# A two-block transformer kernel on one core: the low parts, taps and decays of both mixers in another order, and edits in attention, the first feed-forward head and the last norm

## The reference, cut to what matters

```
xn = rms_norm(h); z = xn @ w_in                       # first block
y_conf = silu(layer_norm(conv31(a * sigmoid(b)))) @ w_conf_pw
y_att  = forgetting_attention(q, k, v, f_logit)       # 4 heads, causal, decay by cumsum(log f)
y_sc   = sc_b * conv3(sc_c * sc_h);  y_pool = window means (2, 4, 8, 16) @ w_pool * scale
h = h + rms_norm(concat(y_conf, y_att, y_sc, y_pool) @ w_out)
h = h + rms_norm(square(relu(rms_norm(h) @ w_up)) @ w_down)          # "ff", 4096 wide
h = h + rms_norm((p @ w_ple_proj) * sigmoid(rms_norm(h) @ w_ple_gate))

x = x + attention_mixer(rms_norm(x))    # 8 latent heads and 4 pairs of differential maps
x = x + swiglu(rms_norm(x))             # "f0", 2816 wide
x = x + recurrent_mixer(rms_norm(x))    # chunked state space (8 heads) and gated linear recurrence (4 heads)
x = x + swiglu(rms_norm(x))             # "f1"
return rms_norm(x)
```

## Time and profile before

| | |
|---|---|
| median of 3 runs | 1001.95 us (999.59 to 1003.36) |
| the profiled execution's own time | 1000.06 us |
| its span (first to last instruction) | 998.2 us |
| TensorE busy | 953.5 us, 96% |
| VectorE, ScalarE, POOL busy | 700.3, 515.8, 87.1 us |
| DMA | 164.40 MB, mean 165 GB/s; the queue of the weights busy for 48.9% of 16 engines |
| a load of 1 MB (w_up, s_w_out), issue to landing | 5.6, 4.9 us |
| an output store of 256 KB | 2.1 us |
| mean granted TensorE clock | 0.992 of full |

### The profile page before, as it was taken

One profiled execution on the slowest core, in us unless ns is written; L12 is line 12 of the kernel. 1 busy time (PEld: TensorE's weight loads), 2 busy tenths in 40 slices (PEclk: granted clock), 3 DMA queues, 4 the chain that ended last, 5 costly groups with the idle time before them and its releaser, 6 DMA issues.

```text
span 998.2 us, 13575 instructions
## 1 busy us (share of the span) xinstructions
PE 953.5 (96%) x5540; PEld 835.9 (84%) x5540; DVE 700.3 (70%) x921; ACT 515.8 (52%) x698; POOL 87.1 (9%) x110
## 2 busy tenths in 40 slices
PE   6997999999999899889999999999989889999997
PEld 5996797888888688778988888888988789888886
DVE  4798785666667887886666666667979676666663
ACT  4776754444436646765543434368645355434341
POOL 4353000000000100000000000000132000000000
PEclk9999999999999999989999999999999999999999
DMA  9732365665565354224665656546321356656531
GB/s 320 245 128 92 120 220 194 199 207 183 174 206 175 112 171 143 85 85 125 215 208 173 207 171 209 169 149 211 127 85 49 121 169 211 207 172 208 172 127 43
DMA packets 106190, 164.40 MB, mean 165 GB/s; under 512 B 2816, under 2 KB 82784, under 8 KB 106000
## 3 DMA queue, kind: packets, MB, share of 16 engines
q1 hardware_dynamic: 104688, 158.25, 48.9%
q0 software_dynamic: 1440, 5.28, 1.5%
HBM read 162.47 MB, written 1.05 MB: 164 GB/s over the span
## 4 chain that ended last, share of the span: by engine, by line
PE 69%; DVE 19%; ACT 6%; issue 4%; DMA 2%; POOL 1%; DVEq 0%; POOLq 0%; ACTq 0%
PE ps L379 67%; DVE wl L1739 6%; DVE SC L1841 2%; PE ps L387 2%; ACT wh L1172 2%; DMA raw<-in_w_in 1%; DVE xhl L1744 1%; DVE xf L1748 1%; ACT junk L1160 1%; DVE st L2139 1%; ACT xhl L1178 1%; POOL st L2496 1%; DVE rows L2339 1%; DVE hs L1759 0%; DVE h L1801 0%
## 5 line engine op out<-in xcount | busy, mean ns | idle before, releaser
L1739 DVE TENSOR_TENSOR wl<-raw,wh 128x2048 fp32r<-128x2048 f32 (+2 forms) x150 | 339.6, 2266 | 153.8 <-ACT wh L1172 153.6
L1172 ACT ACTIVATE wh<-raw 128x2048 fp32r<-128x2048 f32 (+2 forms) x150 | 281.9, 1884 | 156.6 <-PE ps L379 142.8
L379 PE MATMUL ps<-xhl,wh 128*128 128x512 f32 (+1 forms) x1248 | 257.9, 354 | 2.5 <-ACT wh L1237 2.5
L379 PEld LDWEIGHTS ps<-xhl,wh 128*128 128x128 f32 x1248 | 202.4, 193 | 29.9 <-issue 3.7
L379 PE MATMUL ps<-wh,xhl 128*128 128x512 f32 (+3 forms) x1000 | 195.2, 339 | 6.0 <-ACT SC L1435 1.8
L379 PEld LDWEIGHTS ps<-wh,xhl 128*128 128x128 f32 x1000 | 155.1, 190 | 25.3 <-ACT xhl L1178 2.6
L379 PEld LDWEIGHTS ps<-xhl,wl 128*128 128x128 f32 x1008 | 135.6, 191 | 7.5
L379 PE MATMUL ps<-xhl,wl 128*128 128x256 f32 x1008 | 140.6, 282 | 0.0
L379 PE MATMUL ps<-wl,xhl 128*128 128x512 f32 (+3 forms) x500 | 105.2, 336 | 0.0
L379 PE MATMUL ps<-wh,fh 128*128 128x512 f32 x304 | 91.0, 392 | 1.8 <-DVE fl L1986 1.5
L379 PE MATMUL ps<-wh,fl 128*128 128x512 f32 x304 | 90.2, 390 | 0.0
(11 more groups left out here) (266 smaller groups left out, 840.8 us busy)
## 6 DMA issues: line engine op xcount, KB each, us to landing
raw<-in_ffn_gate SPq DMA_DIRECT2D x22, 1024.0 KB, 5.3
raw<-in_ffn_up SPq DMA_DIRECT2D x22, 1024.0 KB, 5.4
raw<-in_ffn_down SPq DMA_DIRECT2D x22, 1024.0 KB, 4.9
raw<-in_w_up SPq DMA_DIRECT2D x16, 1024.0 KB, 5.6
raw<-in_w_down SPq DMA_DIRECT2D x16, 1024.0 KB, 4.9
raw<-in_s_w_in SPq DMA_DIRECT2D x14, 1024.0 KB, 5.4
raw<-in_w_in SPq DMA_DIRECT2D x9, 1024.0 KB, 7.1
raw<-in_a_w_in SPq DMA_DIRECT2D x6, 1024.0 KB, 5.1
```

Of the source, the lines that this page charges most:

```text
L379: return e.matmul(o, a, b, start=start, stop=stop, skip_group_check=True)
L1172: e.activation(high_of(i), raw_of(i), ACT.Copy).then_inc(*up("act_high", i))
L1739: e.tensor_tensor(low_of(i), raw_of(i), high_of(i).bitcast(F32), ALU.subtract).then_inc(*up("dve_lo", i))
```

## The change

Nothing is computed otherwise except in two places: the copies of `xs` and `cbs` go from ScalarE to VectorE, and the last norm multiplies by the gain first and by the root second, the second half of the width on ScalarE. The rest moves steps within an engine's list and changes some waits:

- First mixer. ScalarE: `highs(10)` behind `forget_probs(0)` and `(1)`; taps 22 and 23 before them; the last taps before `forget_turned(0)`; the conformer's Sqrt before `forget_probs(3)`. VectorE: `lows(8)` behind the first maxima, `forget_inverse(0)` and `(1)` before taps 16 to 18, `lows(10)` behind all taps and behind `forget_max(3)`; the conformer's centring and square before `mix_low(3)`.
- `ff` head. TensorE: `down_block(0, 0)` in two halves of the width with a `head_turn` between them, and the turns of slots 6 and 7 ahead of `down_block(0, 1)`. VectorE: one `lows` behind `head_block(1)`, one behind all `head_turned`.
- Attention. `logits(8)` waits for round 0 of the turned copies; ScalarE's tick 7 stands between the rounds; VectorE's `lows(S["aout"][3])` from tick 8 to tick 10.
- Recurrent mixer. TensorE: the second `hq` slot behind the turns of `xs` and the products of `cb`. ScalarE: first `hq` Silu, decay 0 and 1, seg 0, second `hq` Silu, seg 1. VectorE: the four copies, `decayed(0)`, then the waits for `hq`. POOL: `part(2)` waits for `weigh(1)`. Output projection: `lows` of slots sout 2, sout 3 and of the next feed-forward behind the steps of the norms; ScalarE fetches high parts of the next feed-forward between them; `project_end` takes the wait for the low part of the activations only ahead of their product.

```diff
             def project_end(n, sl, tb, half, order, x_low=None):
                     for x in (xh, xl):
+                        if x is xl and i == order[2] and x_low:
+                            e.wait_ge(*x_low)
...
-                    down_block(0, 0)
+                    down_block(0, 0, (0,))
+                    e.wait_ge(*at("dve_head", l, 1, 0))
+                    head_turn(1, 0, 4, 7)
+                    down_block(0, 0, (1,))
                     e.wait_ge(*at("dve_head", l, 1, 1))
-                    head_turn(1, 0, 4, 7)
                     head_turn(1, 4, 2, 2)
-                    e.wait_ge(*at("dve_head_low", l, 1, 4))
-                    down_block(0, 1)
                     head_turn(0, 6, 2, 4)
                     head_turn(1, 6, 2, 5)
+                    e.wait_ge(*at("dve_head_low", l, 1, 0))
+                    down_block(0, 1)
...
                     if i == 8:
+                        e.wait_ge(*at("act_qk_turned", 1, 1, 0))
+                    if i == 9:
                         e.wait_ge(*at("act_qk_turned", 1, 1, 1))
...
-                        e.wait_ge(*at("act_qk_turned", 1, 0, 0))      # map_back(1)
+                        e.wait_ge(*at("act_qk_turned", 0, 0, 1))
...
                 e.wait_ge(*at("act_xbc", 3))                          # TensorE, recurrent
-                feat(S["hq"][1], ps[0])
                 e.wait_ge(*at("act_xb", 3))
...
+                feat(S["hq"][1], ps[0])
                 e.wait_ge(*at("dve_keys", 3))
                 score(8, hk, hq)
...
-                e.wait_ge(*at("dve_mix3_low", 1, 0))
+                e.wait_ge(*at("act_part_high", 6, 1, 0))
                 for half in range(2):
-                    project_end(6, sl, 0, half, order)
+                    project_end(6, sl, 0, half, order, at("dve_mix3_low", 1, 0))
...
-                highs(10)                                             # ScalarE, first mixer
+                taps(22, 24)
                 forget_probs(0)
                 forget_probs(1)
-                taps(22, 26)
+                highs(10)
+                taps(24, 27)
...
-                taps(26, 29)
+                taps(27, TAPS)
...
-                forget_probs(3)
                 e.wait_ge(*at("pe_conf_variance"))
                 e.activation(sg[:, 0:256], ps[1][:, 0:256], ACT.Sqrt, ...)
+                forget_probs(3)
...
-                tick(7, do)                                           # ScalarE, attention, after both rounds
+                    if c == 0:
+                        tick(7, do)
...
+                queries(0)                                            # ScalarE, recurrent
                 decay(0)
-                for tb in range(2): ... e.activation(xs[:, tb, :], ps[(7, 1)[tb]][:, :], ACT.Copy)
                 decay(1)
-                for g in range(2): ... e.activation(cbs[:, g, :], ps[(2, 5)[g]][:, 0:384], ACT.Copy)
                 e.wait_ge(*at("dve_dt_turned"))
                 seg(0)
+                queries(1)
                 seg(1)
...
+                e.wait_ge(*at("dve_mix3_x", 1, 0))
+                part_high(4, 8, 0, (6, 1, 0))
+                highs(UP["f1"][0][0])
+                e.wait_ge(*at("dve_mix3_x", 1, 1))
+                part_high(4, 8, 1, (6, 1, 1))
                 norm_squares(6, 0)
-                highs(UP["f1"][0][0])
+                highs(UP["f1"][0][1])
                 norm_high(6, 0)
...
-                taps(11, 17)                                          # VectorE, first mixer
-                lows(8)
-                taps(17, 20)
+                taps(11, 16)
                 forget_max(0)
                 forget_max(1)
                 forget_bias(3)
-                lows(9)
-                taps(20, 23)
+                lows(8)
                 forget_inverse(0)
                 forget_inverse(1)
+                taps(16, 19)
+                lows(9)
                 (short_in)
-                taps(23, 25)
+                taps(19, 21)
                 forget_max(2)
-                lows(10)
-                taps(25, TAPS)
+                taps(21, TAPS)
...
-                    if t == 8:                                        # VectorE, attention
+                    if t == 10:
                         lows(S["aout"][3])
...
+                lows(S["xbc"][2] + 4)                                 # VectorE, recurrent
+                (tensor_copy of xs 0, 1 and of cbs 0, 1)
                 lows(S["xbc"][3] + 4)
...
+                decayed(0)
                 e.wait_ge(*at("act_hq", 1))
                 weigh(0)
                 weigh(1)
+                decayed(1)
                 e.wait_ge(*at("dma_hm"))
                 score(8)
-                e.wait_ge(*at("act_cb", 1))
-                decayed(0)
-                decayed(1)
                 weigh(2)
...
                 state_out(1)
-                lows(S["sout"][2])
                 state_columns(0)
                 state_low(0)
                 gated_mean(0)
+                gated_mean(1)
                 state_columns(1)
-                gated_mean(1)
+                gated_out(0)
                 state_low(1)
-                for tb in range(2): gated_out(tb)
+                gated_out(1)
+                gated_columns(0)
+                lows(S["sout"][2])
+                gated_columns_low(0)
                 lows(S["sout"][3])
-                for tb in range(2): gated_columns(tb)
+                lows(UP["f1"][0][0])
+                gated_columns(1)
+                gated_columns_low(1)
                 residual(6, 0)
                 norm_rows(6, 0)
-                lows(UP["f1"][0][0])
                 norm_low(6, 0)
+                residual(6, 1)
                 lows(UP["f1"][0][1])
-                residual(6, 1)
+                norm_mean(6, 1)
                 lows(UP["f1"][1][0])
-                norm_mean(6, 1)
+                norm_scale(6, 1)
                 lows(UP["f1"][1][1])
-                norm_scale(6, 1)
...
-                    e.wait_ge(*at("dve_weighed", n - 2))              # POOL, part(n)
+                    e.wait_ge(*at("dve_weighed", max(1, n - 2)))
```

More of the change, by code:

```diff
@@ L480, in project_half, with project_end @@
                 d.then_inc(*(up("pe_slot", sl[i]) if (tb, half) == (1, 1) else up("pe_sums", n, tb, half)))
-            def project_end(n, sl, tb, half, order):
+            def project_end(n, sl, tb, half, order, x_low=None):
                 s, c, o = tokens(tb), HALF[half], ps[ACC[n][tb][half]][:, :]
@@ L671, in head_turn, with down_block @@
                     d.then_inc(*up("pe_head_turned", l, tb, t0))
-                def down_block(j, tb):
+                def down_block(j, tb, halves=(0, 1)):
                     x = [y[:, j % 3, :].rearrange("p (k n) -> p k n", k=2) for y in (fh, fl)]
-                    tok(down[j], [(ps[ACC[s_next][tb][c]][:, :], HALF[c]) for c in range(2)], tb, 0, j == 0, False, x)
+                    tok(down[j], [(ps[ACC[s_next][tb][c]][:, :], HALF[c]) for c in halves], tb, 0, j == 0, False, x)
                 def down_end(tb, half):
@@ L1326, in first_mixer @@
                         *up("act_short_tap", t))
-                taps(29, TAPS)
                 forget_exp(2)
@@ L1646, in recurrent, with queries @@
                 conv_silu(3)
-                for i in range(2):
+                def queries(i):
                     e.wait_ge(*at("pe_slot", S["hq"][i]))
@@ L1663, in seg @@
                         *up("act_seg", i))
+                queries(0)
                 decay(0)
-                for tb in range(2):
-                    e.wait_ge(*at("pe_xs", tb))
-                    e.activation(xs[:, tb, :], ps[(7, 1)[tb]][:, :], ACT.Copy).then_inc(*up("act_xs", tb))
                 decay(1)
-                for g in range(2):
-                    e.wait_ge(*at("pe_cb", g))
-                    e.activation(cbs[:, g, :], ps[(2, 5)[g]][:, 0:384], ACT.Copy).then_inc(*up("act_cb", g))
                 e.wait_ge(*at("dve_dt_turned"))
                 seg(0)
+                queries(1)
                 seg(1)
@@ L1707, in recurrent @@
                 highs(S["sout"][3])
-                for tb in range(2):
-                    e.wait_ge(*at("dve_mix3_x", 1, tb))
-                    part_high(4, 8, tb, (6, 1, tb))
+                e.wait_ge(*at("dve_mix3_x", 1, 0))
[3 more added lines that the diff above has]
+                part_high(4, 8, 1, (6, 1, 1))
                 norm_squares(6, 0)
-                highs(UP["f1"][0][0])
+                highs(UP["f1"][0][1])
                 norm_high(6, 0)
@@ L1725, in scalar @@
             ffn("f1")
-            norm_squares(7, 0)
-            norm_squares(7, 1)
+            for tb in range(2):
+                norm_squares(7, tb)
+                e.wait_ge(*at("pool_rstd", "norm", 7, tb))
+                e.wait_ge(*at("dve_final", tb, 1))
+                e.activation(hs[:, tb, HALF[1]], hs[:, tb, HALF[1]], ACT.Identity, scale=st[:, 3 * tb + 2:3 * tb + 3]).then_inc(
```

(27 more changed lines are left out.)

12 lines of the change are left out of this document (5 added, 7 removed).

## The result

The changed kernel takes 987.13 us (median of 4 runs, 987.02 to 987.38), the kernel before 1000.97 in the four runs beside it (999.59 to 1003.36): ratio 0.986, 95% interval 0.9838 to 0.9881. The forecast was 991.2 with a range of 987.5 to 996.5: the sign was right, the gain forecast was too small (10.7 against 13.8 by the medians), and the time is 0.4 under the range. The profiled execution took 987.16, its span is 985.3 against 998.2, so the two traces differ by 12.9, and 2.2 of the 4.1 us missed lie in them; the rest is the base: I held the sum against 1001.95, while the execution behind the rows took 1000.06.

What follows compares the result with a forecast made beforehand. TensorE, busy 96% of the span, was taken as the bound, with only its idle time and lower-clock stretches to win. Six terms summed to -10.7 against the 1001.95 median: 991.2 us, own range 987.5 to 994.5, with rivals 987.5 to 996.5.

Steps and rivals of the forecast that it cites:

- First mixer, -3.0: Conformer and forgetting attention: reordered taps, highs and lows shorten TensorE's waits; worked out -3.3, taken -3.0 us, ends -1.0 and -4.5.
- Head, -0.6: First feed-forward's start: TensorE's 1.53 us wait for head_low(1, 4) shrinks, next feature block 0.6 us earlier, ends 0 and -1.5.
- Attention, -0.6: Waits before map_logits(8) and map_mix(5) shrink, but the moved lows delays max(10): -0.6 us stays, ends -2.5 and +2.
- rival 3: Attention: two waits of about 2 us keep TensorE's clock at half up to the projection; 1004.3 us, chance 0.06.
- Levels, -2.0: Recurrent mixer: turning xs and cb first brings heads(0) and weigh(2) earlier; -2.0 us, ends -3.0 and +0.5.
- Projection, -4.5: Recurrent mixer's output projection: four TensorE waits of 5.09 us go, two new ones come; -4.5 us, ends -5.5 and -2.0.
- Last norm, 0: End of the kernel: gain first, scaling split over ScalarE and VectorE, stores issued together; 0 us, ends -0.4 and +0.4.
- 1 (VectorE the true bound of both mixers): Both mixers: steps leaving VectorE's queue ahead of a step come back behind it; 996.4 us, chance 0.18.
- 2: Recurrent mixer's levels: the Silu table load waits with its activation, hq(1) 1.28 us later; 992.5 us, chance 0.10.

## Why the prediction was wrong, step by step

- **First mixer, -3.0: the step that failed.** It measured -4.7 by the timelines and -4.9 by the medians. The mechanism held: no wait and no half clock before the turned probabilities, one of 2.56 before the mean (said: about 3), released by VectorE, the last tap at 84.17 (said: 84.8). Two sizes were off. The chain to project(3) moved by 3.2 (said: 2.2; highs(11): 86.81 against 89.99): POOL ended at 81.27, not near 82, the ten taps took 0.66 us each on the whole, and lows(8), for which I had added 0.5 beside POOL, took its 2.28. project(3) itself moved by 2.82 only. It stands without a wait behind TensorE's own work, and the same rows from the mean on took 4.7 us, where they took 3.0 before: the half clock behind the mean's wait, which the sum doesn't have. And behind project(3) I counted only the 1.12 of the earlier trace rows; the timelines there shortened by 1.9. All of it lies around two waits, this one and one of 0.31 that I had not put into the sum: start to start they gave 1.39 and 0.56, each some 0.25 more than its idle entry. Then I cut the worked-out 3.3 to 3.0 for a wait I had not seen; there was none.
- **Head, -0.6:** 0.8 and 1.1. The wait fell from 1.53 to 0.70, as worked out, or a little better.
- **Attention, -0.6:** the size is right by the medians (-0.3) though the timelines say -1.2, and it is partly luck, since a large loss was left out. logits(8) came without a wait, and gain was lost ahead of max(10), as said. But counted from the turned q and k, TensorE's lead over the kernel before was 5.6 us at the turn ahead of the wait (418.79), still 2.6 at turn(9) behind it, and nothing at 429.59: the rows between took 5.3 us at half clock, where the kernel before ran them at full in 2.7. That is rival 3's mechanism, which the sum had only in its upper end. 1.3 came back, since the kernel before stands 0.45, 0.19 and 0.19 us ahead of its projection. And the reason given, a VectorE queue that sets the pace as a whole from there on, is wrong: the same lows at tick 7 gives 2.1 us.
- **Levels, -2.0:** 1.5 and 1.7. The queue of ScalarE, the early table load and heads(0) went as said; relative to the stage's start heads(0) gained 3.0. weigh(2), on its own shift, started 1.95 earlier (said: 2.2), but its first half took 1.42 beside POOL's part(3), against 0.68 in the earlier trace rows; for that I had allowed 0.2. weigh(3), behind it, was 1.2 earlier.
- **Projection, -4.5:** 5.0 and 5.6. All four waits as read, and of the two new ones, 0.25 and 0.4, the first was 0.37 and the second 0.1. By idle entries this gives 4.6; start to start it is 5.0, as in the first mixer.
- **Last norm, 0:** right within its ends of 0.4, though POOL's root, put at 0.55, took 0.93.
- **The base:** the second step that failed. The difference was held against a median of three runs that lay 1.9 above the execution whose rows were summed. With a fourth run the median was 1000.97, and three later medians of the same kernel were 999.31, 1000.92 and 1000.63; the profiled execution with its 1000.06 was the better base. Against it this is 1.9 of the 4.1 us, against the 1000.97 beside the changed kernel 1.0, with 3.1 left to the terms. With the base at 1000.06 the forecast is 989.4 and the range, moved by as much, 985.6 to 994.6, which holds the measured time.
- **The range:** 987.5 to 994.5 does not follow from the terms' ends. Added as independent errors they give 988.3 to 996.1.
- **Rivals.** 1 (VectorE the true bound of both mixers) is out: the mixers' gains stayed, and filling TensorE's wait gave 2.8 more. 2 is out by the load at 721.01. The Trainium skill (ScalarE: Activation LUTs, "What ACT_TABLE_LOAD costs") gives 2.66 us for a switch, a load of 1.28 and a drain of 1.38. The trace agrees with the load alone: each of the three took 1.28, the activation before each ended within 0.02 us of its start, and the load at 721.01 was done 2.6 us before its activation could start. 3 didn't come at its size: the low clock behind turn(9)'s wait ended before 430, but it took 2.6 us of lead, as said above.

## What to carry to other kernels

When a low-priority step is moved out of a critical queue, look for the place where that engine itself waits, not for a later place in the full queue: the same step of 2.28 us at tick 7 instead of tick 10 gave 2 us. An idle stretch of TensorE can cost more than its length, by half clock behind it and by some 0.25 us start to start, so compare the starts of the rows on both sides and not the idle entries. And hold the sum against the execution whose rows were summed.

## What the runs showed of the hardware that was not expected

Whether half clock follows a wait is not told by the wait's length. I had argued from the earlier trace rows that TensorE stood through 86 to 88 at full clock; the same first-mixer order in the kernel with that part undone, after a wait of 2.82 instead of 3.06, ran the next 6 us at half:

```profile
86.00:88.00 2.00, 0.00 (x0) 0.00 (x0) 1.96 (x3) 0.00 (x0) 1.71 (x3) 0.91 0.00 0
88.00:90.00 2.00, 1.73 (x4) 1.50 (x5) 1.70 (x4) 0.92 (x3) 0.17 (x1) 0.50 0.00 0
90.00:92.00 2.00, 2.00 (x10) 1.91 (x10) 0.00 (x0) 2.00 (x3) 0.00 (x0) 0.50 0.00 0
92.00:94.00 2.00, 2.00 (x8) 1.56 (x7) 1.95 (x4) 1.18 (x4) 0.00 (x0) 0.50 0.00 0
```

Its norm_turn(1, 0) came at 119.42 against 118.75. With the new order the same row lay between 113.5 and 114.7 in nine traces. So here one trace gave a stage with long waits to about 0.6 us, and two of them a difference to about 1; for terms below that only repeated times decide, as in attention.
